# Expert lists from products of one-hot matrices, and a last stage without GpSimd

## What is computed

```python
x  = x + (sigmoid(ga) * a + sigmoid(gb) * b) @ w_out
h  = rms_norm(x, g_ffn)                          # per row: x * rsqrt(mean(x*x) + 1e-6) * g
g_sel = argmax(h @ w_rg + b_rg)                  # one of 4 groups
top_v, top_i = top_k(expert logits of g_sel, 2)  # two of its 8 experts
top_w = softmax(top_v) * g_prob
x  = x + sum over the two experts of top_w * (silu(h @ w_g[e]) * (h @ w_u[e])) @ w_d[e]
y  = rms_norm(x, g_final)
```

## Time and profile before

| | us |
|---|---|
| median of 3 runs | 1339.54 (1336.98 to 1339.65) |
| the profiled execution, its own time | 1338.37 |
| its span in the trace | 1336.6 |
| PE busy | 1264.2 (95%) |
| DVE busy | 928.5 (69%) |
| ACT busy | 498.4 (37%) |
| POOL busy | 481.5 (36%) |

### The profile page before, as it was taken

The page is one execution under the profiler, slowest core; times in us unless marked ns, Lnnn a source line. Parts: engine busy times, 40 slices in busy tenths (PEclk is TensorE's granted clock), DMA queues, the critical chain, the costliest instruction groups (busy, mean ns, idle before and its releaser), DMA issues.

```text
span 1336.6 us, 21305 instructions
## 1 busy us (share of the span) xinstructions
PE 1264.2 (95%) x7533; PEld 1098.9 (82%) x7533; DVE 928.5 (69%) x2190; ACT 498.4 (37%) x1074; POOL 481.5 (36%) x768
## 2 busy tenths in 40 slices
PE   5999999999989999998999998999999979999985
PEld 5999999999979999997777766999788758877742
DVE  5665888888899998854777775342656558777636
ACT  5554222122212113224665553000422237665533
POOL 5801595968884116643000010210012234333314
PEclk9999999999999999998999999999999989999998
DMA  7201232121213221103000231843222258999757
GB/s 258 72 27 42 78 85 81 37 79 38 70 36 123 96 67 56 28 1 100 1 16 2 67 100 50 297 149 135 111 96 79 79 203 301 348 341 342 298 196 317
DMA packets 79312, 163.78 MB, mean 123 GB/s; under 512 B 12529, under 2 KB 47937, under 8 KB 78065
## 3 DMA queue, kind: packets, MB, share of 16 engines
q1 hardware_dynamic: 65121, 129.31, 28.4%
q0 software_dynamic: 12656, 27.62, 6.1%
q10 hardware_dynamic: 1440, 5.58, 1.1%
HBM read 137.81 MB, written 39.21 MB: 132 GB/s over the span
## 4 chain that ended last, share of the span: by engine, by line
PE 78%; DMA 8%; POOL 5%; ACT 3%; DVE 3%; issue 2%; SPq 1%; POOLq 0%; ACTq 0%; DVEq 0%
PE bank L876 11%; PE bank L875 11%; PE bank L877 11%; PE bank L1085 4%; DMA region_h<-in_wd 4%; PE bank L1160 3%; PE bank L1267 3%; PE bank L1154 3%; PE bank L1003 2%; PE bank L1067 2%; PE bank L1172 2%; PE bank L1171 2%; PE bank L1173 2%; DMA region_t<-ffn_input_scratch,small_i 2%; PE bank L1156 2%
## 5 line engine op out<-in xcount | busy, mean ns | idle before, releaser
L1858 DVE MAX8 small<-region_kv 128x8 f32<-128x272 f32 (+4 forms) x241 | 190.2, 828 | 47.6 <-DVE region_kv L1863 47.5
L875 PE MATMUL bank<-h_hi,w_hi 128*128 128x384 f32 (+1 forms) x576 | 196.1, 340 | 0.0
L876 PE MATMUL bank<-h_lo,w_hi 128*128 128x384 f32 (+1 forms) x576 | 196.1, 340 | 0.0
L1863 DVE MATCH_REPLACE8 region_kv<-small,region_kv 128x272 f32<-128x272 f32 (+4 forms) x241 | 195.5, 818 | 0.0
L877 PE MATMUL bank<-h_hi,w_lo 128*128 128x384 f32 (+1 forms) x576 | 194.4, 338 | 0.0
L2189 POOL TENSOR_TENSOR w_lo<-w_stage,w_hi 128x512 fp32r<-128x512 f32 x64 | 80.8, 1299 | 144.8 <-ACT w_hi L1371 144.7
L875 PE MATMUL bank<-w_hi,h_hi 128*128 128x256 f32 x448 | 128.9, 288 | 2.3 <-ACT region_q L1434 2.3
L877 PE MATMUL bank<-w_hi,h_lo 128*128 128x256 f32 x448 | 125.9, 281 | 0.0
L876 PE MATMUL bank<-w_lo,h_hi 128*128 128x256 f32 x448 | 125.9, 281 | 0.0
L877 PEld LDWEIGHTS bank<-h_hi,w_lo 128*128 128x128 f32 x576 | 108.7, 189 | 0.0
L876 PEld LDWEIGHTS bank<-h_lo,w_hi 128*128 128x128 f32 x576 | 108.2, 188 | 0.6
(11 more groups left out here) (328 smaller groups left out, 3114.5 us busy)
## 6 DMA issues: line engine op xcount, KB each, us to landing
w_stage<-in_w_in SPq DMA_DIRECT2D x72, 256.0 KB, 3.2
region_kv<-in_xa SPq DMA_DIRECT2D x16, 512.0 KB, 5.8
region_q<-in_wg SPq DMA_DIRECT2D x12, 512.0 KB, 7.1
region_q<-in_wu SPq DMA_DIRECT2D x12, 512.0 KB, 19.4
region_q<-in_wd SPq DMA_DIRECT2D x12, 512.0 KB, 22.8
region_w<-in_wg SPq DMA_DIRECT2D x10, 512.0 KB, 7.1
region_w<-in_wu SPq DMA_DIRECT2D x10, 512.0 KB, 19.5
region_w<-in_wd SPq DMA_DIRECT2D x10, 512.0 KB, 22.6
```

Of the source, the lines that this page charges most:

```text
L875: mm(out, st_hi(k), mv_hi(k), start=(k == 0), stop=False)
L876: mm(out, st_hi(k), mv_lo(k), start=False, stop=False)
L1858: nc.vector.max(m8[:, q, :], x).then_inc(dve_c, 1)
L1863: nc.vector.match_replace(x, m8[:, q, :], x, TAKEN).then_inc(dve_c, 1)
```

## The change

**Lists.** A second product makes the heads on the chip. `place(t)` compares each row's rank in its expert with the numbers 0 to 127 (`r_at_place`, 128x128, one for each of the two choices); `route(t)` multiplies the one-hot of the expert with the pair (entry number minus SENT, weight) (`r_entry`, 128x64, two buffers). PE multiplies the two for both choices and accumulates over all tiles in bank 2 (`listing`). DVE adds SENT to what comes out and has `heads`, and `gidx` from it. The scatters to DRAM remain, for the overflow branch alone: those of the last tile are issued behind the first three gathers, and nothing before that branch waits for them. The constants that this needs (0 to 127 and the entries) are loaded into `nbuf` by one more DMA when attention is over.

**The last rows of h2.** Those of tile 8 are no longer made by DVE and stored by SP. POOL multiplies x2 with `gffn` (`h2_last`), ACT scales by the row's factor and issues the store itself, in front of its two exponentials for that tile. SP is thus free to issue the weights of experts 3, 4 and 5 as soon as the out-projection is done; those of expert 6 wait for the first gather. WARM is 7.

**Last stage.** For odd tiles ACT no longer copies: it squares each half straight from its bank, the second half first (PE makes the halves in that order now), adds EPS to the sum of that half by a one-column instruction, and takes the square root of the total with ACT's Sqrt. DVE takes the reciprocal and multiplies, for odd tiles in two halves from the banks. POOL has no work there.

The number of unread products, and PE:

```diff
-WARM = 14
+WARM = 7
...
+            def listing(t):
+                pe.wait_ge(list_ready, t + 1)
+                for q in range(2):
+                    last = mm(bank[2][:, 0:2 * NE], r_at_place[:, q, :], r_entry[:, t % 2, q, :], start=(t == 0 and q == 0),
+                              stop=(t == NT - 1 and q == 1), skip_group_check=True)
+                last.then_inc(listed, 1)
...
             for t in range(1, NT):
                 pe.wait_ge(m_high, t + 1)
                 pe.wait_ge(m_low, t + 1)
+                if t >= 3:
+                    listing(t - 3)
                 out_half(t, 0, 0, KD)
...
                     k1 = 6
                     rank(t - 1)
+                    listing(t - 2)
                 x2_trans(t, 0)
                 out_half(t, 1, k1, KD)
             x2_trans(NT - 1, 1)
             logits(NT - 1)
+            listing(NT - 2)
             rank(NT - 1)
+            listing(NT - 1)
```

ACT, behind `norm2(NT - 1)`:

```diff
+                    act.wait_ge(rstd_ready, NT)
+                    act.wait_ge(h2_scaled, 1)
+                    nc.scalar.activation(h2_last, h2_last, ACT.Copy, scale=tnrm[:, NT - 1, 1:2]).then_inc(h2_ready, 1)
+                    act.wait_ge(h2_ready, NT)
+                    act.dma_start(h2_d[(NT - 1) * P:NT * P, :], h2_last).then_inc(h2_out[(NT - 1) % 2], 16)
                     route_exp(t - 1)
```

ACT, last stage:

```diff
+            nc.scalar.activation(froot[:, NT, :], eps_col, ACT.Sqrt)
...
+                    for hf in (1, 0):
+                        act.wait_ge(y1_pe, t + 1 - hf)
+                        nc.scalar.activation(fsq[:, t % 2, hf * 512:(hf + 1) * 512], bank[t - 1 + hf][:, :], ACT.Square,
+                                             scale=1.0 / 32.0, accum_out=fnrm[:, t, hf:hf + 1]).then_inc(fms_ready, 1)
+                        n_ms += 1
+                        if hf == 1:
+                            act.wait_ge(fms_ready, n_ms)
+                            offset = fnrm[:, t, 1:2]
+                            nc.scalar.activation(offset, offset, ACT.Identity, bias=eps_col).then_inc(fms_ready, 1)
+                            n_ms += 1
+                act.wait_ge(fms_ready, n_ms)
+                nc.scalar.activation(froot[:, t, :], fnrm[:, t, 0:1], ACT.Sqrt, bias=offset).then_inc(frstd_ready, 1)
```

DVE, in `route(t)`:

```diff
+                if t >= 2:
+                    dve.wait_ge(listed, t - 1)
+                for q in range(2):
+                    tt(r_entry[:, t % 2, q, :].rearrange("p (e w) -> p e w", w=2),
+                       r_oh[:, t, q * NE:(q + 1) * NE].unsqueeze(2).to_broadcast([P, NE, 2]),
+                       pairs[:, t, q, :].unsqueeze(1).to_broadcast([P, NE, 2]), ALU.mult)
```

DVE, in `place(t)`:

```diff
+                if t >= 1:
+                    dve.wait_ge(listed, t)
+                for q in range(2):
+                    last = ts(r_at_place[:, q, :], place_iota, r_rank[:, t, q:q + 1], None, ALU.is_equal)
+                last.then_inc(list_ready, 1)
+                nc.vector.tensor_copy(entry_w[:, t, :, 1], pairs[:, t, :, 1])
```

DVE, behind `place(NT - 1)`:

```diff
-            h2_of(NT - 1)
+            dve.wait_ge(listed, NT)
+            found = bank[2][:, 0:2 * NE].rearrange("p (e w) -> p e w", w=2)
+            link(ts(heads[:, :, 0], found[:, :, 0], float(SENT), None, ALU.add))
+            ts(gidx, heads[:, :, 0], 1, None, ALU.logical_shift_right).then_inc(gidx_ready, 1)
```

DVE, in `final(t)`:

```diff
+                link(nc.vector.reciprocal(froot[:, t, :], froot[:, t, :]))
```

POOL:

```diff
-                    pool.wait_ge(ms_ready, t + 1)
-                    rstd(tnrm, t).then_inc(rstd_ready, 1)
+                if t == NT - 1:
+                    pool.wait_ge(x2_ready, 2 * NT)
+                    tt(h2_last, x2[:, t, :], gffn, ALU.mult).then_inc(h2_scaled, 1)
+                pool.wait_ge(ms_ready, t + 1)
+                rstd(tnrm, t).then_inc(rstd_ready, 1)
+            list_out(NT - 2)
...
             for e in range(3):
                 gather(hg[:, e, :], gidx[:, e:e + 1], hg_in[e])
+            list_out(NT - 1)
...
-            for t in range(NT):
-                pool.wait_ge(fms_ready, t + 1)
-                rstd(fnrm, t).then_inc(frstd_ready, 1)
```

More of the change, by code:

```diff
@@ L235, in build @@
         vjunk = sm(1)
+        eps_col = sm(1)
+        froot = sm(NT + 1, 1)
         pjunk = sm(3)
@@ L379, in build @@
         r_oh = nflat[:, 0:NT * 2 * NE].rearrange("p (t e) -> p t e", t=NT)
+        place_iota = nflat[:, 576:576 + P]
+        pairs = view(nflat, 576 + P, NT, 4).rearrange("p t (q w) -> p t q w", q=2)
+        r_at_place = view(nflat, 740, 2, P)
+        r_entry = view(nflat, 996, 2, 2, 2 * NE)
+        h2_last = RT[:, 2048:3072]
         r_if = rtile(NT, 2)
@@ L650, in build @@
         list_init = sem("lists_initialised")
+        list_ready = sem("list_entries_ready")
+        listed = sem("list_entries_placed")
+        h2_scaled = sem("last_rows_weighted")
         scattered = sem("lists_scattered")
-        cnt_done = sem("counts_done")
         over_ready = sem("overflow_table_ready")
@@ L823, in _ @@
             load_e(0)
-            for t in range(NT):
+            for t in range(NT - 1):
                 if t in (3, 6):
@@ L827, in _ @@
                     load_e(t // 3)
-                if t == NT - 1:
-                    sp.wait_ge(o7_done, 2 * NT)
-                    load_e(3)
                 sp.wait_ge(h2_ready, t + 1)
                 sp.dma_start(h2_d[t * P:(t + 1) * P, :], h2[:, t % 2, :]).then_inc(h2_out[t % 2], 16)
-            sp.wait_ge(scattered, 16 * 2 * NT)
-            sp.dma_start(heads[:, :, :], lists[0:P, :, :]).then_inc(lidx_in, 16)
-            for e in range(4, NSLOT):
+            sp.wait_ge(o7_done, 2 * NT)
+            for e in range(3, NSLOT - 1):
                 load_e(e)
+            sp.wait_ge(hg_in[0], 16)
+            load_e(NSLOT - 1)
             sp.wait_ge(over_ready, 1)
@@ L1237, in _ @@
             logits(NT - 1)
+            listing(NT - 2)
             rank(NT - 1)
+            listing(NT - 1)
             pe.wait_ge(pos_ready, NT)
[L1240 removed]
+            mm(bank[1][:, P:P + NE], onesb, onehots[:, NT, :], start=True, stop=True).then_inc(rank_done, 1)
             for i in range(WARM):
@@ L2088, in _ @@
             nc.vector.tensor_copy(over_i[:, 1:2], f_cum[:, NE * OVER_J - 1:NE * OVER_J]).then_inc(over_ready, 1)
-            dve.wait_ge(lidx_in, 16)
-            ts(gidx, heads[:, :, 0], 1, None, ALU.logical_shift_right).then_inc(gidx_ready, 1)
             def act_of(par):
@@ L2155, in final @@
                 dve.wait_ge(frstd_ready, t + 1)
-                stt(out=x2[:, t, :], in0=x2[:, t, :], scalar=fnrm[:, t, 1:2], in1=gfin,
-                    op0=ALU.mult, op1=ALU.mult).then_inc(fin_ready, 1)
+                link(nc.vector.reciprocal(froot[:, t, :], froot[:, t, :]))
+                if t % 2 == 0:
+                    stt(out=x2[:, t, :], in0=x2[:, t, :], scalar=froot[:, t, :], in1=gfin,
+                        op0=ALU.mult, op1=ALU.mult).then_inc(fin_ready, 1)
+                    return
+                for hf in range(2):
+                    cs = slice(hf * 512, (hf + 1) * 512)
+                    last = stt(out=x2[:, t, cs], in0=bank[t - 1 + hf][:, :], scalar=froot[:, t, :], in1=gfin[:, cs],
+                               op0=ALU.mult, op1=ALU.mult)
+                last.then_inc(fin_ready, 1)
             combine(0)
@@ L2368, in _, with list_out @@
                 tt(wao_lo[c % 3][:, :, :], wao_raw[c % 3], wao_hi[c % 3][:, :, :].bitcast(F32), ALU.subtract).then_inc(wao_low, 1)
-            for t in range(NT + 2):
+            def list_out(t):
+                pool.wait_ge(pos_ready, t + 1)
+                for q in range(2):
+                    pool.indirect_dma_start(out=list_d, in_=entries[:, t, q, :], in_offset=None,
+                                            out_offset=bass.IndirectOffsetOnAxis(ap=posi[:, t, q:q + 1], axis=0)
+                                            ).then_inc(scattered, 16)
+            for t in range(NT):
                 if t == 2:
@@ L2373, in _ @@
                 if t >= 2:
-                    pool.wait_ge(pos_ready, t - 1)
-                    for q in range(2):
-                        pool.indirect_dma_start(out=list_d, in_=entries[:, t - 2, q, :], in_offset=None,
-                                                out_offset=bass.IndirectOffsetOnAxis(ap=posi[:, t - 2, q:q + 1], axis=0)
-                                                ).then_inc(scattered, 16)
-                if t < NT:
-                    pool.wait_ge(ms_ready, t + 1)
-                    rstd(tnrm, t).then_inc(rstd_ready, 1)
+                    list_out(t - 2)
+                if t == NT - 1:
[4 more added lines that the diff above has]
+            list_out(NT - 2)
             def gather(dst, idx, s):
@@ L2441, in _constants @@
     pos += [CACHE + np.tile(np.arange(DEC_S), DEC_B)]
-    c = np.zeros((P, K_END), np.float32)
+    c = np.zeros((P, K_ALL), np.float32)
     c[:, K_ID:K_ID + P] = np.eye(P)
```

42 lines of the change are left out of this document (21 added, 21 removed).

## The result

| | before | after |
|---|---|---|
| median, first comparison | 1339.60 (4 runs, 1336.98 to 1340.09) | 1328.54 (4 runs, 1328.42 to 1328.95) |
| ratio, 95% interval | | 0.9922 [0.9905, 0.9939] |
| the profiled execution, its own time | 1338.37 | 1328.54 |
| its span | 1336.6 | 1326.7 |
| the same, a later comparison | 1335.21 (9 runs) | 1328.43 (5 runs), ratio 0.9950 [0.9936, 0.9963] |

What follows compares the result with a forecast made beforehand. Bounds: PE in the out-projection, the chain of waits at the turn, the experts moving with their first, then the last-stage chain. 3.15 - 8.25 - 2.65 = -7.75 us from 1338.37 gave 1330.6; forecast 1331.0, range 1327 to 1336.5.

Steps and rivals of the forecast that it cites:

- Step 1: Out-projection: seven listings at 0.45 us each on PE's full path, +3.15 us; bounds 3.15 and 12.2.
- the far one (1.74): Out-projection: upper price of one listing, 1.74 us for four records, from records of 512 columns.
- rival (b): Out-projection: PE and DVE wait for each other at the listings, making the kernel slower, up to 1343.9; chance 0.07.
- Step 2: Turn to the experts: first gather starts at 1076.2 instead of 1081.10, -4.9 us; last rows' store taken to land at 1075.
- rival (a): Turn: the last rows' store waits behind all nine loads, so gathered rows come late; 1336.7, half of it 1334.7; chance 0.20.
- Step 3: Turn: unread products, ending after the gather's landing, put e_trans(0) at 1083.7 instead of 1090.22, -6.5 us.
- Step 4: First expert: PE comes straight from the unread products, so its clock stays high, -1.75 us.
- Step 5: Last stage: DVE's last `final` ends at 1327.45 instead of 1330.10, -2.65 us; bounds 1.0 and 3.5.
- The root's table: Last stage: Sqrt needs one table load of 1.28 us, in ACT's idle time before the first squares, costing nothing.
- The sign named for this step: Last stage: from PE's last product to DVE's end 4.4 us instead of 7.1.
- 6.5 us more pass to the end of the span; those stay.: Program end: the 6.5 us after DVE's last `final` were taken to remain unchanged.
- Rival (c): Expert stage, full of DMA, ends when its bytes are through, so the list change does nothing: 1338.9; chance 0.07.

Runs made afterwards that it cites:

- rows_early: The changed kernel, DVE's table not waiting for the last store, loads of experts 4 to 6 behind the first gathered rows, 4 unread products instead of 7: 1325.96 us.
- warm14: The changed kernel with 14 unread products at the turn instead of 7: 1332.44 us.
- warm1: The changed kernel with 1 unread product at the turn instead of 7: 1327.55 us.
- last_only: The kernel before with only the new last stage (root on ACT, reciprocal on DVE, nothing on POOL): 1330.70 us.
- fill0: The changed kernel without the 11 unread products that PE makes ahead of the last stage: 1326.89 us.
- after_again: The changed kernel itself, unaltered, measured again in a later comparison: 1328.43 us, ratio 0.9950 to the kernel before.
- lists_only: The changed kernel with the last stage of the kernel before, so the list change alone: 1331.95 us.
- pool_tail: The changed kernel, with POOL waiting for DVE's last `final` and then clearing one scratch column: 1333.16 us.

## Why the prediction was right, and where it wasn't

**Step 1, listings, +3.15.** Right: 0.43 us for the listing in a tile (14.43 against 14.00), 0.40 on the mean of the seven (2.8 in all), and 0.45 for a doubled one, where 0.45 was said. The low bound by the nearest row was the price, the far one (1.74) nowhere near, and the waits stayed covered, so rival (b) had no ground.

**Step 2, first gather -4.9.** `gidx` was there 11.3 us after the last residual began (said: 11.4). The store didn't land at 1075 of the prediction's clock but at 1077.5, near its late bound of 1078.6, 8.3 us after its issue. The gather started 2.8 us earlier, not 4.9. What rival (a) needed was thus nearly there. rows_early shows the queued loads as the cause: 3.2 us without those of two of the three experts. The Trainium skill (DMA: Bandwidth & Descriptors, "Queues, rings and completion order") lets each DMA engine take turns between queues that have work; by that the store would, as an estimate, have taken about twice its 2.6 us. With 7.8 to 8.6 us in the ten traces with these loads this isn't borne out as the prediction used it.

**Step 3, e_trans(0) -6.5.** Measured, on the same clock, 1082.9 instead of 1083.7: -7.3. Two errors cancelled. The late gather landed in about 4.2 us, not in 6.4, since the loads had meanwhile thinned out (DMA share 1.03 in 1078 to 1080, 0.48 in 1082 to 1084), so the rows were there at 1082.5 where 1082.6 was said. That is luck. The 14 records took 8.5 us from 1074.6 (said: 8.7 from 1075.0). That the unread products can decide is shown by warm14 (+5.5); with one of them (warm1) the rows land at the same moment, so after stands at the point where both end together.

**Step 4, clock, -1.75.** Right in mechanism, too large in size: -1.0. The stretch from gate and up of expert 0 to that of expert 1 shrank by 1.4 us (6.29 to 4.88), since the third part of gate and up took 1.20 us before and after, where the step put it at 0.96 at the high clock; and PE waited 1.28 us for ACT's copy, where 0.82 before and 0.8 in the step stood, which costs 0.4. That the turn as a whole, forecast at -8.25, measured -8.3 is this shortfall of 0.75 against 0.8 more in step 3, and so luck to that extent. warm1 takes the unread products away and the low clock is back. Not foreseen: before pays this cost only in some executions (last_only's turn was 3 us shorter with the same code), so the gain depends on the run of before beside it.

**Step 5, last stage, -2.65.** The edit by itself was sized well: -3.2 in last_only, -2.9 in fill0. In the change it was -0.75, below the bound of 1.0. The failed piece is "I laid its instructions one behind another": combine(8) was taken to start when DVE was free, and its rows weren't there, because 22 more product records, each with a weight load, pushed PE's code into one block more, fetched in a stage with full DMA engines. Nothing in the prediction looked at code. Without that block the step's own path is there: combine(8) at 25.7 us after the first load and DVE's end at 34.0 in fill0, 25.7 and 34.2 on the prediction's clock. The root's table was as said: one load of 1.28 us at 1281.44, and 11.67 us of idle time before the first squares. The sign named for this step, 4.4 us from PE's last product to DVE's end, says little: it was 5.3 in after, 6.3 in after_again and 4.4 in fill0, and DVE didn't wait for PE's last product in after.

**"6.5 us more pass to the end of the span; those stay."** Wrong, by 3.2 us. It was read as the last store's way home; that is 3.3 us. The rest was POOL's drain, 7.5 us behind its last power, and the change takes POOL out of the stage. SP's 3.6 us at the closing barrier stood in the trace of before.

So the 2.5 us between 1331.0 and 1328.54 are: 3.2 of this, less 1.9 of step 5, and 0.35 of the listings, 0.35 upstream, 0.1 in the experts and 0.4 by which the forecast was put above its own sum. The forecast owes its closeness in part to two errors of opposite sign. Rival (c), bound by transfers, was wrong as argued: the experts took 194.8 and 194.7 us. The low end of the range doesn't follow from the terms given for it: 1338.4 + 3.15 - 8.25 - 3.5 - 1.5 is 1328.3, not 1327, and the measured 1328.54 lies close to that.

## What to carry to other kernels

Read the end of a program like a stage of its own: an engine that works late and is slow to close (POOL) can end behind the last store, and a barrier's wait may be put down to an engine that had long been done. Where the DMA engines are full, ask who else uses them: here a block of PE's code cost 2 us of rows, and 44 instructions fewer or 56 more took that away. A small store that the next stage waits for goes ahead of bulk loads: in rows_early expert 4's were issued at 1083.6, still 17 us before ACT first read them (1101.2).

## What the hardware showed that I had not expected

POOL's closing drain ends 7.5 us after POOL's last instruction does, in all 14 traces, be that a power (before, lists_only) or a clearing of 0.1 us; those of PE, DVE and ACT end within 0.1 us of theirs. SP's wait at the closing barrier was 0.2 us in after, 3.6 in before and 4.8 in pool_tail, by when POOL was through.

A fetch of 16 KB of code took 1.1 us beside full DMA engines, and behind it one of a tile's 16 parts landed 1.3 us after the others, of the last tile 2.3 us, while the other 15 were in time. That this part belongs to the DMA engine that made the fetch is inferred from these times; the trace doesn't name the engine.

Loads of 1 MB in the last stage land every 2.49 us (421 GB/s) behind a first at +4.7, and tile 8's rows were at +25.4 or later in all 14 traces, whatever the engines did; the last stage waits for bytes up to combine(8) (DVE began it within 0.03 us of the landing in all traces but before's and those of the two kernels that put `final` of tile 5 ahead).
